# First attention of block 1 in pairs of heads, its value product behind queries and keys, and every gate product in the fused form

## The reference, cut to what matters

```python
h = rms_norm(x, mix_norm_g[l])
proj = h @ w_in[l]
sb_q, sb_k, sb_v, sw_q, sw_k, sw_v, gate_logits = jnp.split(proj, split_at, axis=-1)
# stick-breaking attention, 8 heads of 64
log_keep = jnp.where(strict, -jax.nn.softplus(z), 0.0)
tail = lax.cumsum(log_keep, axis=3, reverse=True) - log_keep
w = jnp.where(strict, jnp.exp(jax.nn.log_sigmoid(z) + tail), 0.0)
...
gates = jax.nn.sigmoid(gate_logits)              # 2 x 1024 columns: 16 tiles of 128
merged = gates[:, :, 0] * y_sb + gates[:, :, 1] * y_swa
x = x + merged @ w_out[l]
```

## Time and profile before

| what | us |
| --- | --- |
| median of 3 runs | 2334.74 (2334.29 to 2335.71) |
| the profiled execution's own time | 2335.98 |
| its span in the trace | 2334.3 |
| TensorE busy in the span | 2280.2 |
| VectorE busy | 1489.5 |
| ScalarE busy | 1157.4 |

### The profile page before, as it was taken

How to read it: one execution, slowest core, us unless ns; L and a number is a source line. 1 busy time by engine, 2 the same in 40 slices (tenths; PEclk the granted TensorE clock), 3 DMA queues, 4 the chain that set the end, 5 groups by cost and what they waited for, 6 DMA issues and landing times.

```text
span 2334.3 us, 35415 instructions
## 1 busy us (share of the span) xinstructions
PE 2280.2 (98%) x14356; PEld 2015.2 (86%) x14370; DVE 1489.5 (64%) x2026; ACT 1157.4 (50%) x1785; POOL 198.3 (8%) x191
## 2 busy tenths in 40 slices
PE   7999999999999999999999999999999999999998
PEld 6898888888888888799999878888888999987887
DVE  4557855646874775665667677668655665776774
ACT  4845444574543544545443554445444445355543
POOL 0001200001110210000004001011100000220110
PEclk9999999999999999999999999999999999999999
DMA  7335565533666665554534555566655444364654
GB/s 227 110 115 175 186 201 179 156 112 123 192 189 197 215 191 191 175 177 153 164 100 151 184 165 188 189 208 199 190 175 184 161 158 126 104 215 148 186 185 140
DMA packets 108995, 395.73 MB, mean 170 GB/s; under 512 B 12375, under 2 KB 12545, under 8 KB 108577
## 3 DMA queue, kind: packets, MB, share of 16 engines
q1 hardware_dynamic: 104400, 377.53, 50.7%
q0 software_dynamic: 4432, 15.93, 2.1%
HBM read 392.92 MB, written 1.05 MB: 169 GB/s over the span
## 4 chain that ended last, share of the span: by engine, by line
PE 92%; ACT 4%; DVE 2%; issue 1%; DMA 1%; SPq 0%; DVEq 0%; ACTq 0%
PE psum L409 55%; PE psum L538 17%; PE psum L537 9%; PE psum L837 3%; PE psum L871 2%; PE psum L762 2%; PE psum L855 1%; DMA ring<-in_weights 1%; ACT w_high L363 1%; DVE w_low L366 1%; PE psum L1879 1%; ACT L1338 0%; DVE xT L721 0%; ACT xT L715 0%; DVE x L630 0%
## 5 line engine op out<-in xcount | busy, mean ns | idle before, releaser
L366 DVE TENSOR_TENSOR w_low<-ring,w_high 128x1024 fp32r<-128x1024 f32 x704 | 863.6, 1237 | 512.3 <-ACT w_high L363 510.5
L363 ACT ACTIVATE w_high<-ring 128x1024 fp32r<-128x1024 f32 x704 | 734.5, 1055 | 484.9 <-DMA ring<-in_weights 483.6
L538 PE MATMUL psum<-xT,w_high 128*128 128x512 f32 x1728 | 607.5, 396 | 0.0
L537 PE MATMUL psum<-xT,w_low 128*128 128x256 f32 x1728 | 485.4, 281 | 0.0
L409 PE MATMUL psum<-xT,w_high 128*128 128x256 f32 x2496 | 462.4, 287 | 0.0
L409 PEld LDWEIGHTS psum<-xT,w_high 128*128 128x128 f32 x2496 | 391.6, 193 | 0.8
L538 PEld LDWEIGHTS psum<-xT,w_high 128*128 128x128 f32 x1728 | 324.2, 188 | 77.6
L409 PE MATMUL psum<-w_high,hidden 128*128 128x512 f32 x1216 | 376.7, 390 | 0.0
L409 PE MATMUL psum<-xT,w_low 128*128 128x256 f32 x1248 | 354.4, 284 | 0.0
L537 PEld LDWEIGHTS psum<-xT,w_low 128*128 128x128 f32 x1728 | 326.5, 189 | 0.2
L409 PEld LDWEIGHTS psum<-w_high,hidden 128*128 128x128 f32 x1216 | 228.2, 188 | 47.2
(11 more groups left out here) (237 smaller groups left out, 2309.7 us busy)
## 6 DMA issues: line engine op xcount, KB each, us to landing
ring<-in_weights SPq DMA_DIRECT2D x706, 512.0 KB, 3.6
pages<-in_affine POOLq DMA_DIRECT2D x16, 512.0 KB, 5.8
ring<-in_weights SPq DMA_DIRECT2D x8, 440.0 KB, 3.2
pages<-in_gains POOLq DMA_DIRECT2D x4, 512.0 KB, 4.8
pages<-in_mem POOLq DMA_DIRECT2D x2, 1024.0 KB, 5.6
ring<-in_weights SPq DMA_DIRECT2D x4, 384.0 KB, 3.1
x<-in_x_in SPq DMA_DIRECT2D x2, 512.0 KB, 4.8
pages<-in_rows POOLq DMA_DIRECT2D x2, 512.0 KB, 5.8
```

Of the source, the lines that this page charges most:

```text
L363: eng.activation(high, raw, ACT.Copy).then_inc(self.flag("w_rounded").sem, 1)
L366: eng.tensor_tensor(self.w_low[:, piece % SLOTS, 0:width], raw, high.bitcast(F32), ALU.subtract).then_inc(self.flag("w_split").sem, 1)
L537: pe.matmul(out[:, 0:SEQ], low, self.xT_high[:, k, :], start=(k == 0), stop=False, skip_group_check=True)
L538: m = pe.matmul(out, high, self.xT[:, k, :, :].rearrange("p x s -> p (x s)"), start=False, stop=(k == kn - 1), skip_group_check=True)
```

## The change

Five edits. (1) In block 1 the product `sbv` (the values of the first attention) moves behind `sbq` and `sbk`. (2) Its heads are taken in pairs on all engines. (3) Softplus is one ACT instruction, where it was three; the VectorE step behind it takes the maximum where it added, since softplus is whole now. (4) All 96 gate tiles go through `gemm_beside`: VectorE adds the halves into SBUF, and ACT's Tanh reads and writes SBUF and counts a new flag `gate_ready`. (5) Of block 1's gates eight lie within the loop over heads and gate 8 behind it; gate 9 takes gate 11's place, and gates 10 to 13 lie beside the window attention, in steps 1, 3, 5 and 6. VectorE's work for the window heads (`window_heads`) is cut into smaller parts and starts earlier.

```diff
-BESIDE_SWA = {0: [("ysb", 1)], 1: [("gate", 12)], 2: [("ysb", 2)], 4: [("ysb", 3)], 6: [("gate", 13)]}
+BESIDE_SWA = {0: [("ysb", 1)], 1: [("gate", 10)], 2: [("ysb", 2)], 3: [("gate", 11)], 4: [("ysb", 3)],
+              5: [("gate", 12)], 6: [("gate", 13)]}
...
-            c.gemm_tokens(pe, l, stream, banks, "sbv", xT, KD, 512)
             for key in ("sbq", "sbk"):
                 for n in range(2):
                     c.gemm_features(pe, l, stream, banks, key, (key, n), xTf, KD, [(key, 2 * n), (key, 2 * n + 1)])
+            c.gemm_tokens(pe, l, stream, banks, "sbv", xT, KD, 512)
...
             def gate(n):
-                c.gemm_features(pe, l, stream, banks, "gate", ("gate", n), xTf, KD, [("gate", n)])
-
-            for h in range(10):
-                if h < 8:
-                    logits(h)
-                if 1 <= h <= 8:
-                    later_keys(h - 1)
-                if h < 9:
-                    for n in GATES_SB[h]:
-                        gate(n)
-                if h >= 2:
-                    sb_values(h - 2)
-            gate(10)
+                c.gemm_beside(pe, l, stream, banks, ("gate", n), xTf, KD, ("gate", n))
+
+            for h in range(0, 8, 2):
+                for x in (h, h + 1):
+                    logits(x)
+                if h:
+                    for x in (h - 2, h - 1):
+                        sb_values(x)
+                gate(h)
+                for x in (h, h + 1):
+                    later_keys(x)
+                gate(h + 1)
+            for x in (6, 7):
+                sb_values(x)
+            gate(8)
...
-                b = soft[:, h % 2, 0:SEQ + P]
-                act.activation(b, c.psum[:, 4 + h % 2, 0:SEQ + P], ACT.Abs).then_inc(*c.flag("act_step").one())
-                c.settle(act, l, "act_step")
-                act.activation(b, b, ACT.Exp, scale=-1.0).then_inc(*c.flag("act_step").one())
-                c.settle(act, l, "act_step")
-                act.activation(b, b, ACT.Ln, bias=1.0).then_inc(*c.flag("sb_ln").one())
+                act.activation(soft[:, h % 2, 0:SEQ + P], c.psum[:, 4 + h % 2, 0:SEQ + P], ACT.Softplus
+                               ).then_inc(*c.flag("sb_soft").one())
...
             def gate(n):
-                act.activation(gates[:, n, :], c.filled(act, l, banks, ("gate", n))[:, 0:SEQ], ACT.Tanh, scale=0.5
-                               ).then_inc(*c.drained(banks, ("gate", n)))
+                c.wait_drained(act, l, banks, ("gate", n))
+                act.activation(gates[:, n, :], gates[:, n, :], ACT.Tanh, scale=0.5).then_inc(*c.flag("gate_ready").one())
                 after(("gate", n))
...
+            def gate(n):
+                c.halves_added(dve, l, banks, ("gate", n), gates[:, n, :])
+                after(("gate", n))
```

More of the change, by code:

```diff
@@ L1073, in block_1 @@
     banks, BOTH = Banks(), ("act", "dve")
-    for key in ("swq", "swkv", "sbv"):
+    for key in ("swq", "swkv"):
         for t in range(NT):
             banks.add((key, t))
-    for key, first, end in (("sbq", 0, 2), ("sbk", 0, 2), ("gate", 0, 12), ("ysb", 0, 2), ("gate", 12, 13), ("ysb", 2, 4),
-                            ("gate", 13, 16), ("ysw", 0, 4)):
+    for key, first, end in (("sbq", 0, 2), ("sbk", 0, 2), ("sbv", 0, 2), ("gate", 0, 10), ("ysb", 0, 2), ("gate", 10, 11), ("ysb", 2, 3),
+                            ("gate", 11, 12), ("ysb", 3, 4), ("gate", 12, 16), ("ysw", 0, 4)):
         for n in range(first, end):
@@ L1305, in _ @@
             after("swkv")
[L1306 to L1310, removed]
             after(("sbq", 0))
@@ L1321, in _ @@
             c.root(act, l, c.fac[:, :, 0:2])
+            split(c.piece_after["sbv"] + AHEAD - 1)
+            for t in range(NT):
+                act.activation(sbv[:, t, :], c.filled(act, l, banks, ("sbv", t)), ACT.Copy
+                               ).then_inc(*c.drained(banks, ("sbv", t)))
             def softplus(h):
@@ new lines, in _ @@
+            for n in range(2):
+                after(("sbk", n))
+                next(side)
+            next(side)
+            split(c.piece_after["sbv"] + AHEAD - 1)
+            def gate(n):
+                c.halves_added(dve, l, banks, ("gate", n), gates[:, n, :])
+                after(("gate", n))
+            for h in range(0, 8, 2):
+                for x in (h, h + 1):
+                    dve.wait_ge(*c.flag("sb_soft").at(l, x + 1))
+                    if h:
+                        dve.wait_ge(*c.flag("sb_summed").at(l, x - 1))
+                    dve.scalar_tensor_tensor(kept[:, x % 2, 0:SEQ + P], c.psum[:, 4 + x % 2, 0:SEQ + P], 0.0,
+                                             soft[:, x % 2, 0:SEQ + P], ALU.max, ALU.max
+                                             ).then_inc(*c.flag("sb_kept").one())
+                if h:
+                    gate(h - 1)
+                else:
+                    after("sbv")
@@ L1491, in _ @@
                 next(side, None)
+                gate(h)
+                next(side, None)
+            gate(7)
             for _ in side:
                 pass
-            after(("gate", 9))
             c.settle(dve, l, "dve_step")
@@ L1504, in _ @@
                             ).then_inc(*c.read_out("dve", "swq0"))
-            after(("gate", 11))
+            gate(9)
             c.turned(dve, l, "swk")
```

146 lines of the change are left out of this document (79 added, 67 removed).

## The result

The changed kernel takes **2346.44 us** (median of 6 runs, 2345.06 to 2347.12), beside 2335.22 us (6 runs, 2330.41 to 2338.92) of the kernel before. The ratio is 1.005, with a 95% interval of 1.0039 to 1.0061: slower by half a per cent, where 2314.8 us was forecast. The profiled execution took 2346.66 us, with a span of 2344.9.

The account below looks back on a forecast made before the run. TensorE, busy 2280 of 2334 us, was taken to bound the kernel. Gains 16.2 + 3.4 + 4.0 less 2.7 and 1.0 make 19.9 us: 2335.98 to 2316.1, median 2314.8 us; eight-in-ten range 2307 to 2324.

Parts of the forecast that it names:

- first attention: Block 1: TensorE's waits go, 8.5 - 1.0 us in layer 0 and 9.7 - 1.0 in layer 1, 16.2 us gained.
- window attention: Block 1: gates 10 and 11 moved there fill TensorE's waits in steps 3 and 5, 3.4 us gained over two layers.
- fused form: Gate tiles of both blocks: 0.042 us saved per tile, 4.0 us over 96 tiles.
- late copies: Block 1: window-key copy and parts of `osw` come late behind gates 9 and 14, 2.7 us lost over two layers.
- pairs' logits: Block 1's first attention: logits of successive pairs start 10.6 to 10.8 us apart, a sign the forecast is right.
- Softplus: Block 1's first attention, on ACT: taken as one pass, 0.49 us; upper bound the three passes it replaces, 1.54.
- (a): End of block 1's first attention: transposes wait for copies late in VectorE's queue, 1.0 us per layer.
- (b): Block 1, behind gate 9: the copy of the window keys gets 0.69 us later, taken as 0.7.
- (c): Block 1, behind gate 14: the parts of `osw`, just late already, get 0.65 us later.
- Block 2's attentions: Halves wait for the gate; side work and maxima come 0.69 us later; cost 0.5 us per layer, 1.0 in all.
- upper bound: Block 2's attentions: 0.69 us lost in all 16 units with gates of both layers, 22 us.
- Rival 5: VectorE's 0.69 us shows in all 40 units with gates of both blocks, 28 us, giving 2342 us; chance 0.04.

Follow-up runs that it names:

- the run with block 1 alone: The changed kernel with block 2 as it was before the change (two 256-column passes, Tanh straight out of the bank): 2319.18 us, ratio 0.9934.
- the run with the rounding first: The changed kernel, but in block 2 ScalarE rounds the next piece of weights before it takes a gate's Tanh: 2313.91 us, ratio 0.9913.
- the run with three passes: The kernel with weights rounded before Tanh in both blocks, but each pair's Softplus made as Abs, Exp and Ln again: 2314.12 us.
- the best one: The changed kernel with weights rounded before each gate's Tanh in block 1 as well as block 2: 2309.11 us, ratio 0.9892.
- the run with block 2 alone: The kernel before with block 2 alone as changed (gates fused, VectorE adds the halves, Tanh reads its sum): 2362.31 us, ratio 1.0115.
- the run with Softplus alone: The kernel before with one edit, Abs, Exp and Ln of block 1's first attention made one Softplus: 2327.59 us, ratio 0.9965.

## Why the prediction was wrong

**Right: block 1.** The forecast has 16.2 for the first attention, 3.4 for the window attention, 1.3 of the fused form and 2.7 of late copies against them: some 18.2. The trace shows 17.4; the medians 15.0 (12.6 to 18.4 by the interval). The pairs' logits were to start 10.6 to 10.8 us apart; the steady ones do so by 10.87. Softplus was taken at one pass, 0.49, and is 0.49:

```profile
L1330 ACT ACTIVATE pages<-psum 128x384 f32<-128x384 f32 x8 | 3.8, 490 | 3.6 <-PE psum L1184 3.6
L1337 ACT ACTIVATE pages<-psum 128x384 f32<-128x384 f32 x8 | 3.9, 492 | 8.0 <-PE psum L1192 8.0
```

The Trainium skill (ScalarE: Activation LUTs, "Step-by-step: what each stage is for") states that every function costs the same for an element; Softplus at 490 ns and Exp at 492 agree with it. The waits (a), (b) and (c) were forecast at 1.0, 0.7 and 0.65 us:

```profile
116.67 1.53 PE L764 MATMUL psum<-ident,pages 128*128 128x128 f32 x12 [0.64 <-DVE pages L1513]
...
125.41 0.38 PE L834 MATMUL psum<-masks,identb 128*128 128x512 bf16 x1 [0.91 <-DVE pages L1522]
...
169.30 0.48 PE L411 MATMUL psum<-rounded_pages,w_high 128*128 128x256 f32 x2 [0.86 <-issue]
```

They are 2.41 us a layer against 2.35. Their places were right, each size came within 0.4 us and the sum by offsetting errors, and their cause was right only in part: I gave 0.69 us of added work, and the run with the order mended in block 1 shows that they go while the work stays.

**Right, and undersized: the fused form.** Block 2 has 64 tiles, for which the forecast has 2.7 us; the run with block 1 alone against the one with the rounding first gives 5.3, and the attentions of layer 0 take 281.18 us in the one and 278.70 in the other, both without a stretch at the lower clock. In an MLA unit two gates take 5.83 us from their start to the next form's start before, and 5.63 in the run with the rounding first:

```profile
1078.20 0.36 PE L539 MATMUL psum<-xT,w_low 128*128 128x256 f32 x1
...
1083.83 0.38 PE L839 MATMUL psum<-pages 96*128 96x256 f32 x1
```

So a tile saves up to 0.1 there, not 0.042: I took the tile inside an unbroken stream. An estimate by the Trainium skill (TensorE: Matmul & The Clock Gate, "Back-to-back issue gap"), from an isolated matmul's 2.5 ns of overhead, gives 1.3 us for the 64 tiles. The page gives this formula for a single matmul and not for a stream, and the runs, with 5.3 us, are four times above it.

**Wrong: "Block 2's attentions".** The step reads: "The halves wait for the gate in VectorE's order, and the side work and maxima behind them come later by 0.69." That takes the addition as one delay, paid once. It is a link in a ring through two in-order queues, and each round of the ring costs again. VectorE comes to gate 1 at 1054.42, some 2.4 us behind its product, in the changed kernel; with the rounding first it comes as late, but has caught up by gate 3, where it waits for TensorE. In the ring it can't: two gates and their copies take it 7.9 us (1062.32 to 1070.21), where TensorE needs 7.4, and the first maximum is 5.2 late. Then a unit has 10.0 us that had 8.6. I took 0.5 us a layer, and 22 us for both layers as the upper bound; the attentions took 14.6 and 12.9 us more in the traces, 17.1 and 17.0 more than in the same kernel with the ring open. The bound was too low for the same reason, and it counted nothing for the lower clock behind such waits, about 4 us a layer.

**Rival 5 was nearly it, and was argued away.** It named the condition, "only if the delay of one unit is passed on to the next", the view that would show it (transposes that wait for exponentials) and 2342 us; it came out at 2346.4. The argument against it was a sum of durations: exponentials, Tanh, rounding, `w_low` and maximum take 5.0 us of 5.4, "with the reduction beside the exponentials". A sum of durations for one gate in a unit misses two things: units 0, 1, 2 and 6 of MLA have two gates, and between two gates the ring lets nothing stand beside anything. For NSA's units of one gate, from which the sum was drawn, it held better: in layer 0 L857 waits there once, 1.87 us, and 5.3 of the 17.1 us are lost behind MLA, two of the three stretches at the lower clock among them. The ring's period was to be had from the prediction's own figures: halves 0.69, Tanh 0.38, rounding 1.06 and `w_low` 1.24 make 3.37 us, more than the tile's 2.87. The 3.35 measured is that near by chance too: the Tanh with a bias takes 0.51 and not 0.38, but two of the four members start about 0.1 before the one ahead of them ends. The prediction set these figures against the unit, and in another order than that in which each waits for the other.

## What to carry to other kernels

Where a change puts an engine between two others, write down what stands behind each of its instructions in the queues of all three, and look for a ring: its period is the sum of its members' durations, and if that is above the pace of the bounding engine, a small addition costs its surplus in every round. What opens a ring is often an order: here ScalarE's rounding ahead of its Tanh, with no work taken away, made 32.5 us in block 2 and 4.8 in block 1, and turned a change that was slower by 0.5% into one that is faster by 1.1%. Low busy shares (66% and 48%) say nothing against it, since in the ring both engines are idle by waiting for each other.

## What the runs showed of the hardware

Stretches with the same instructions differ by 2 to 4 us between two kernels' executions: from the end of layer 0's attentions in block 2 to the next layer's first products there are 498.1 us in the run with three passes and 500.7 in the best one, and 496.4 in the run with block 2 alone where the changed kernel has 500.1. Within the attentions one reason can be seen. They take 278.7 us in each layer of the run with the rounding first in block 2 and 280.2 in the best kernel, by the same instructions, and only the latter has a stretch at the lower clock there, with no wait ahead of it: TensorE came from 16-column products of the compressed attention (L839) and their transposes. The column before the last two is the granted clock:

```profile
1149.00:1152.40 3.40, 3.40 (x14) 2.79 (x14) 2.75 (x5) 1.17 (x9) 0.00 (x0) 0.50 0.23 89
```

So a difference of one to four microseconds in a single trace is no evidence here by itself; the worth of the fused form in block 1 stays open for that reason.

A table load takes 1283 ns of ScalarE in each kernel, and the function behind it starts at once, here in the run with Softplus alone:

```profile
89.03 1.28 ACT L1334 ACT_TABLE_LOAD   x1
90.32 0.49 ACT L1334 ACTIVATE pages<-psum 128x384 f32<-128x384 f32 x1
```

The load stands between Exp and Ln too, in the kernel before and in pairs of three passes, though Exp stands on both sides of the Ln.
